# Narrower level products in the gated recurrence: stationary columns up to the last key, 64 query columns moving

## What is computed

```python
b = jnp.cumsum(g, axis=1)
diff = jnp.minimum(b[:, :, None] - b[:, None, :], 0.0)
decay = jnp.where(causal[None, :, :, None, None], jnp.exp(diff), 0.0)
scores = jnp.einsum('bthk,bshk,btshk->bhts', q, k, decay)
o = jnp.einsum('bhts,bshv->bthv', scores, v) + jnp.einsum('bthk,bhkv->bthv', q * jnp.exp(b), S0)
```

## Time and profile before

| | us |
|---|---|
| median of 3 runs | 1388.84 (1388.37 to 1389.0) |
| profiled execution, its time | 1389.89 |
| span of that execution in the trace | 1388.1 |
| PE busy in the span | 1349.7 (97%) |
| DVE busy | 901.5 (65%) |
| ACT, POOL busy | 644.4, 677.5 |

### The profile page before, as it was taken

How to read it: one execution, slowest core, us unless ns; L and a number is a source line. 1 busy time by engine, 2 the same in 40 slices (tenths; PEclk the granted TensorE clock), 3 DMA queues, 4 the chain that set the end, 5 groups by cost and what they waited for, 6 DMA issues and landing times.

```text
span 1388.1 us, 21204 instructions
## 1 busy us (share of the span) xinstructions
PE 1349.7 (97%) x8092; PEld 1207.2 (87%) x8092; DVE 901.5 (65%) x1669; ACT 644.4 (46%) x1155; POOL 677.5 (49%) x469
## 2 busy tenths in 40 slices
PE   6999999999998999999999999999999999999998
PEld 6999999999995555468889999999999999999786
DVE  4355556998897865435569484949495858587342
ACT  5455553988756565521135352525253434444121
POOL 2454443846466777720027382828383747464100
PEclk9999999999999999999999999999999999999999
DMA  7211111233225100002231010111111111107222
GB/s 247 83 37 31 32 31 31 78 84 95 69 62 182 31 16 4 32 28 94 81 93 48 17 52 32 41 43 37 47 37 47 37 47 37 47 7 230 85 80 91
DMA packets 101875, 86.80 MB, mean 63 GB/s; under 512 B 6640, under 2 KB 90480, under 8 KB 101776
## 3 DMA queue, kind: packets, MB, share of 16 engines
q1 hardware_dynamic: 100144, 80.63, 19.3%
q0 software_dynamic: 1632, 4.82, 0.9%
HBM read 65.46 MB, written 19.97 MB: 62 GB/s over the span
## 4 chain that ended last, share of the span: by engine, by line
PE 87%; DVE 7%; issue 2%; POOL 2%; ACT 1%; DMA 0%; SPq 0%; DVEq 0%; POOLq 0%; ACTq 0%
PE bank L190 45%; PE wide L1671 7%; PE bank L1568 7%; PE bank L241 6%; PE bank L1109 4%; PE wide L1080 4%; PE wide L720 4%; PE bank L1093 2%; PE wide L454 1%; PE wide L1678 1%; DVE states L1992 1%; PE wide L1681 1%; PE wide L241 1%; POOL probs L1054 1%; DVE o_rec L2036 1%
## 5 line engine op out<-in xcount | busy, mean ns | idle before, releaser
L190 PE MATMUL bank<-hn_hi,rw_hi 128*128 128x352 f32 x768 | 250.5, 326 | 1.6 <-DVE hn_lo L180 1.6
L190 PE MATMUL bank<-hn_hi,rw_lo 128*128 128x352 f32 x768 | 246.7, 321 | 0.0
L190 PE MATMUL bank<-hn_lo,rw_hi 128*128 128x352 f32 x768 | 246.4, 321 | 0.0
L190 PE MATMUL bank<-hn_hi,w_hi 128*128 128x352 f32 x648 | 209.9, 324 | 0.0
L190 PE MATMUL bank<-hn_hi,w_lo 128*128 128x352 f32 x648 | 208.0, 321 | 0.0
L190 PE MATMUL bank<-hn_lo,w_hi 128*128 128x352 f32 x648 | 207.8, 321 | 0.0
L1054 POOL TENSOR_SCALAR probs<-probs,low 128x128 f32<-128x128 f32 (+8 forms) x72 | 131.2, 1828 | 57.1 <-DVE low L1201 56.9
L190 PEld LDWEIGHTS bank<-hn_hi,rw_hi 128*128 128x128 f32 x768 | 144.1, 188 | 3.5 <-issue 3.0
L190 PEld LDWEIGHTS bank<-hn_lo,rw_hi 128*128 128x128 f32 x768 | 144.6, 188 | 0.0
L190 PEld LDWEIGHTS bank<-hn_hi,rw_lo 128*128 128x128 f32 x768 | 144.2, 188 | 0.0
L817 POOL TENSOR_TENSOR swapped<-swapped,sin 128x352 f32<-128x352 f32 x57 | 54.9, 963 | 144.9 <-ACT swapped L759 102.2
(11 more groups left out here) (265 smaller groups left out, 3050.2 us busy)
## 6 DMA issues: line engine op xcount, KB each, us to landing
rw_raw<-in_rec_w_in SPq DMA_DIRECT2D x32, 512.0 KB, 4.1
w_raw<-in_att_w_in SPq DMA_DIRECT2D x27, 512.0 KB, 4.0
xin<-in_x_prompt SPq DMA_DIRECT2D x8, 512.0 KB, 4.5
wo_raw<-in_att_w_out SPq DMA_DIRECT2D x4, 1024.0 KB, 8.5
x_again<-in_x_prompt SPq DMA_DIRECT2D x8, 512.0 KB, 4.2
residual<-h_rows SPq DMA_DIRECT2D x8, 512.0 KB, 2.9
wf_raw<-in_rec_w_out SPq DMA_DIRECT2D x4, 1024.0 KB, 8.8
h_again<-residual SPq DMA_DIRECT2D x8, 512.0 KB, 4.2
```

The source lines that it names most:

```text
L190: last = pe.matmul(out, l, r, start=n == 0, stop=n == len(passes) - 1)
```

## The change

For levels 0 to 5 the stationary operand is cut to the first `r - m` columns of the chunk (the last m tokens of a chunk are queries of a second half, never keys): 64, 96, 112, 120, 124 and 126 columns for levels 0 to 5 instead of 128; 16, 24, 28 and 30 instead of 32 for the sample chunk at levels 2 to 5. The moving operand is only the second halves, `r // 2` columns (64, or 16 for the sample), read as runs of m columns with m left out between them. The result has `r - m` partitions and 64 adjacent columns, and four chunks lie in the first half of a bank. DVE's copy reads them there, on `r - m` partitions; its element count per partition (256) is as before. The numbers of matmuls, of copies, of banks and of waits stay, and the LEVELS product isn't touched.

```diff
-                        left, right = (k[:, slot, at_c], q[:, slot, at_c]) if level == LEVELS else (
-                            levels[:, level, at_c], levels[:, level, at_c])
-                        last = pe.matmul(out[:, 0:r], left, right, start=True, stop=True)
+                        if level == LEVELS:
+                            last = pe.matmul(out[:, 0:r], k[:, slot, at_c], q[:, slot, at_c], start=True, stop=True)
+                        else:
+                            m = P >> (level + 1)
+                            out = wide[0:r - m, i % 4, j * (P // 2):j * (P // 2) + r // 2]
+                            last = pe.matmul(out.rearrange("p (n m) -> p n m", m=m),
+                                             levels[:, level, c * P:c * P + r - m],
+                                             seconds(levels[:, level, at_c], level)[:, :, 1, :], start=True, stop=True)
...
-                        dst = seconds(pairs[0:r, cs, 0:r], level)[:, :, :, 1, :]
-                        mask = seconds(masks[0:r, level, 0:r], level)[:, :, 1, :]
-                        part = wide[0:r, i % 4, :].rearrange("p (c x) -> p c x", x=P)[:, 0:n, 0:r]
-                        part = seconds(part, level)[:, :, :, 1, :]
+                        used = r - m
+                        dst = seconds(pairs[0:used, cs, 0:r], level)[:, :, :, 1, :]
+                        mask = seconds(masks[0:used, level, 0:r], level)[:, :, 1, :]
+                        part = wide[0:used, i % 4, 0:n * P // 2].rearrange("p (c x) -> p c x", x=P // 2)[:, :, 0:r // 2]
+                        part = part.rearrange("p c (n m) -> p c n m", m=m)
                         dve.wait_ge(product_ready, i + 1)
                         dve.wait_ge(dve_read, n_dve[before[g] + 1])
-                        dve.copy_predicated(dst, mask.unsqueeze(1).to_broadcast([r, n, blocks, m]), part).then_inc(dve_read, 1)
+                        dve.copy_predicated(dst, mask.unsqueeze(1).to_broadcast([used, n, blocks, m]), part).then_inc(dve_read, 1)
```

## The result

| | before | changed |
|---|---|---|
| median of the runs, us | 1388.92 | 1374.64 (1373.56 to 1375.89) |
| ratio | 1 | 0.9897, 95% interval 0.988 to 0.9914 |
| profiled execution: time, span | 1389.89, 1388.1 | 1373.6, 1371.8 |
| median in a second comparison | 1388.97 | 1375.81 (1375.6 to 1376.56); 0.9908, 0.9892 to 0.9925 |

The changed kernel is 14.3 us faster in the first comparison and 13.2 in the second; the prediction said 12.4.

A forecast was written before the change was run, and what follows sets the result against it. PE was taken to bound the kernel. Per head 1.69 + 0.21 + 0.06 - 0.15 - 0.26 = 1.55 us, 12.4 in eight, gives a median of 1376.4 us; range 1373.5 to 1385.5.

The forecast's parts named there:

- The bound and the place: PE bounds the kernel; the change touches only eight unbroken pieces of level products, one a head, 98 us.
- what is late next: After the pieces, `out`, projections, DVE's differences and the final product move along, so the gain reaches the end.
- The pace is the longer of load and matmul: Inside the level products, steps fall from 0.111 us to 0.058 to 0.110; 1.69 us a head saved.
- Ends of groups: Uncovered matmuls ahead of four sample groups save 0.21 us a head; shorter lone loads after shape changes save 0.06.
- Change of shape at level 0: 64 columns count as their own shape, so going to level 1 loses 0.15 us a head.
- the wait for DVE: At level 0, group 1, PE waits for DVE's read of the LEVELS product's group 0: 0.26 us a head lost.
- Short runs: Rival, 10%: at levels 3 to 5 short moving runs make the matmul take 0.107 again; 2.8 us lost, 1379.2.
- Load not following: Rival, 12%: full-shape loads don't shrink with columns; only level 0 gains, 1383.2 (7%), or only group ends, 1387.1 (5%).
- The clock: Rival, 5%: PE's clock falls in the levels, 1.7 us a fall; one a head takes the gain, two give 1403.6.

The follow-up runs named there:

- 1: Only the moving half of the change: 128 (sample: 32) stationary columns as in the original, 64 moving ones; median 1390.88 us, ratio 1.0031.
- 2: Only the stationary half of the change: 64 to 126 stationary columns, 128 moving ones as in the original; median 1386.72 us, ratio 0.9994.
- 3: The changed kernel with 66 instead of 64 stationary columns at level 0, giving it level 1's shape class; 1374.81 us, ratio 0.9906.
- 4: The changed kernel, with DVE reading only the first of four chunks of the LEVELS product, group 0, in heads 1 to 7 (outputs differ); 1375.21 us.
- experiment 5: The changed kernel with 66 stationary columns at all levels of the prompt groups (later keys left out, outputs differ); 1351.93 us, one run.
- 10: The changed kernel with the levels run from 5 down to 0; 1390.8 us, from 1383.49 to 1396.57, ratio 1.0017.

## Why the prediction was right, and where it was not

- **The bound and the place.** PE, in eight unbroken pieces: right. The saved time reached the end undiminished; DVE, DMA and the final stage moved along, as the prediction's paragraph on what is late next said. What it calls head 3 is head 4; no number hangs on that.
- **The pace is the longer of load and matmul, and both are linear in columns.** Right to 0.001 us a step at each level, and shown from both sides: 1 leaves 0.111, 2 leaves 0.109 to 0.110, both halves together give 0.058 to 0.110. The sharpest part of the prediction was that halving the moving columns alone gains nothing. The load's price came from the gaps between the first two loads after a change of shape.
- **Ends of groups, 0.21 and 0.06.** Inside the sum they fit: 1.59 measured against 1.55. In 1, where only the shorter tails act, the piece lost 0.26 instead of 0.21.
- **Change of shape at level 0, 0.15, and the wait for DVE, 0.26.** Both gaps are in the trace: 0.09 ahead of the load at 1054.99, and 0.26 between the two groups of level 0. Booking them side by side was not quite right: 3 shows that the first is worth nothing by itself, since the next wait for DVE ends at the same moment. That 64 columns are a shape of their own is shown by 2, where the change costs 0.17; 4 shows that the second is worth 0.26.
- **Short runs (10%).** No cost: 0.059 a step at runs of 2 [experiment 5]. **Load not following (12%).** Out, by the steps above.
- **The clock (5%).** It didn't fall in the pieces of the changed kernel. But this part of the prediction was the weakest. Its price was wrong: a fall was set at 1.7 us, from one in the final product. In a piece of sparse pairs the clock stays down until `out`, 17 to 20 us, and costs 7.5 to 9.4. Two falls in the eight heads, not one a head, would then have been enough to take the gain. And its evidence was no evidence: the clock had stayed up over the stretch from 716.0 to 719.5 and behind it; in the changed kernel the same stretch of work, 712.7 to 716.2, was followed by a fall (0.71). One execution in which a clock stays up says little. Nor did PE stream moving columns for 96% of the piece: 0.107 of 0.1115 is its share of one step, and over the whole piece it is about 86%. That the clock stayed up is in part luck: the order of the levels, which the change left alone and the prediction didn't consider, kept it up here, as 10 shows.
- **The whole.** 12.4 forecast; 14.3 and 13.2 measured, 12.7 of it in the pieces. In the two profiled executions the difference is the kernel's beginning, 3.3 and 1.0 us earlier, and the clock's short falls outside the pieces, of some 1.5 us each. The 12 traces of this case show the fall after the wait for f_lo in 8, and the one near 718 in 5, so both go and come. So I put only the 12.7 and the 0.3 between the pieces down to the change; the medians alone can't part them from the rest.

## What to carry to other kernels

Where every matmul has a weight load of its own, read the step between starts, and get the load's price from the first two loads after a change of shape: below the point where both are equal, only cutting stationary and moving columns together gains. Once PE gets faster, waits for its readers that were covered come out one after the other (level 0's bank, then the LEVELS reads, then `out`); here idle PSUM banks and one shared product were worth as much again as the change. And try the order in which the work comes behind a wait: with the short-stepped pairs last instead of first the clock fell and the gain was gone.

## What the runs showed of the hardware

- Where the load paces, a pair of an fp32 load of c stationary columns and its matmul takes about 0.84 ns x c and 0.004 us: steps of 0.058, 0.084, 0.104 and 0.109 us at 64, 96, 120 and 126 columns. Beside it 64 moving fp32 columns are free, in runs down to 2 (0.059 at 66 stationary columns).
- A step paced by a matmul of 128 fp32 moving columns is 0.109 to 0.110 (experiment 2), one paced by a load of 128 is 0.1115.
- Going from 64 to 96 stationary columns costs 0.17 us where nothing hides it (experiment 2).
- TensorE's clock can fall to 1.2 GHz while the profile shows PE busy all the time (3.00 of 3.00 us, 0.50 granted). It did so where 64 moving columns stood in a step of 0.11 us, and stayed there for 17 to 20 us, until the products of `out`. That I had not expected: the busy time of PE doesn't show this danger. The Trainium skill ("TensorE: Matmul & The Clock Gate", Part 1) names waits and idle gaps as what takes the clock down; here there is hardly an idle gap within the piece, only short waits ahead of it (PE busy for 2.80 and 2.83 of the 3 us before the two falls in head 0).
